# A two-layer mixer/expert kernel on one core: matrices' front with two output buffers, chunk loads in another order, late modulation rows behind the chunks

## What is computed

```python
for i in range(2):                       # layer 0: chunk mixer, layer 1: state-space mixer
    mod_x = silu(c) @ ada_w[i] + ada_b[i]        # six rows of 1024: shift, scale, gate, twice
    mod_c = silu(c_ctx) @ ada_w[i] + ada_b[i]
    xn = rmsnorm(x) * (1 + sc1) + sh1            # cn likewise from the context
    x = x + g1 * mixer(xn)
    x = x + g2 * peer(rmsnorm(x) * (1 + sc2) + sh2)   # 8 heads x 16 experts looked up per token
# state-space mixer: u = xn @ w_in; a diagonal complex scan h_t = a*h_(t-1) + B u_t both ways,
# y = C h + d*u; out = val * sigmoid(gate), [val, gate] = gelu(y) @ w_out
```

## Time and profile before

| | us |
|---|---|
| median of 3 runs (3746.65 to 3755.1) | 3750.82 |
| the profiled execution's own time | 3749.29 |
| its span, first to last instruction | 3747.4 |

### The profile page before, as it was taken

One profiled execution on the slowest core, in us unless ns is written; L12 is line 12 of the kernel. 1 busy time (PEld: TensorE's weight loads), 2 busy tenths in 40 slices (PEclk: granted clock), 3 DMA queues, 4 the chain that ended last, 5 costly groups with the idle time before them and its releaser, 6 DMA issues. The chain is left out here.

```text
span 3747.4 us, 46785 instructions
## 1 busy us (share of the span) xinstructions
PE 3166.1 (84%) x15952; PEld 2087.9 (56%) x15952; DVE 2247.1 (60%) x5038; ACT 1429.8 (38%) x3564; POOL 962.4 (26%) x796
## 2 busy tenths in 40 slices
PE   3886999999988999897766798888877989889897
PEld 2774566554444655442345644444326779777897
DVE  5664766667667666679414466767752259512397
ACT  1222444434334444443224244444432237423275
POOL 0001433434333333344200155444550000000000
PEclk7887999999999999999977899999998989899999
DMA  6746999999999999999967499999992235332353
GB/s 248 277 167 267 418 415 417 421 419 409 421 420 399 409 405 415 415 417 352 369 230 238 163 421 421 421 421 415 415 406 106 90 130 179 135 115 91 129 183 118
DMA packets 177136, 1152.67 MB, mean 308 GB/s; under 512 B 21860, under 2 KB 30264, under 8 KB 43306
## 3 DMA queue, kind: packets, MB, share of 16 engines
q0 software_dynamic: 113936, 827.38, 53.9%
q1 hardware_dynamic: 56058, 304.90, 21.6%
q10 hardware_dynamic: 6944, 17.91, 1.3%
HBM read 1128.86 MB, written 21.25 MB: 307 GB/s over the span
## 5 line engine op out<-in xcount | busy, mean ns | idle before, releaser
L1126 PE MATMUL PS<-AR 128*128 128x512 f32 x3072 | 1511.9, 618 | 249.6 <-ACT AR L1184 241.7
L1311 POOL DMA_INDIRECT AR<-in_peer_uv,AR x768 | 949.2, 1236 | 1514.0 <-PE PS L1126 1109.2
L1287 DVE CUSTOM_DVE_ANT_0 AR<-AR,H 128x1024 f32<-128x1024 f32 x768 | 940.9, 1225 | 655.9 <-DMA AR<-in_peer_uv,AR 636.2
L1126 PEld LDWEIGHTS PS<-AR 128*128 128x128 f32 x3072 | 559.8, 193 | 852.9 <-issue 420.4
L1179 ACT ACTIVATE SM<-SM 128x1 f32<-128x1 f32 x768 | 155.7, 203 | 1130.4 <-DVE SM L1287 1125.3
L1087 PEld LDWEIGHTS PS<-HT,W 128*128 128x128 f32 x1536 | 298.9, 195 | 273.2 <-issue 258.0
L1087 PE MATMUL PS<-HT,W 128*128 128x256 f32 x1536 | 427.6, 387 | 2.7 <-issue 1.3
L1184 ACT ACTIVATE AR<-CON,SM 128x128 f32<-128x128 f32 x768 | 309.1, 402 | 45.6 <-PE PS L1126 21.1
L2578 PE MATMUL PS<-XP,WP 128*128 128x256 f32 x2112 | 264.2, 287 | 22.5 <-DVE WP L2735 15.4
L2578 PEld LDWEIGHTS PS<-XP,WP 128*128 128x128 f32 x2112 | 261.0, 196 | 28.2 <-issue 27.7
L1181 ACT ACTIVATE SM<-SM 128x1 f32<-128x1 f32 x768 | 227.1, 296 | 25.1
(11 more groups left out here) (368 smaller groups left out, 3313.0 us busy)
## 6 DMA issues: line engine op xcount, KB each, us to landing
W<-in_peer_w_q SPq DMA_DIRECT2D x48, 1024.0 KB
W<-in_ada_w SPq DMA_DIRECT2D x32, 1024.0 KB
W<-in_ffn_gate SPq DMA_DIRECT2D x22, 1024.0 KB
W<-in_ffn_val SPq DMA_DIRECT2D x22, 1024.0 KB
W<-in_ffn_out SPq DMA_DIRECT2D x22, 1024.0 KB
W<-in_cm_w_in SPq DMA_DIRECT2D x16, 1024.0 KB
AR<-min_scr SPq DMA_DIRECT2D x16, 1024.0 KB, 9.6
AR<-in_peer_uv,AR POOLq DMA_INDIRECT x768
```

What stands on the lines that cost most here:

```text
L1126: mm = pe.matmul(PS[:, 4 + (u % 2) * 2 + c, :], self.DIAG[:, r % 4, :], self.UV[:, r % RING, D + c * 512:D + (c + 1) * 512], start=(k == 0 ...
L1287: v.tensor_tensor_reduce(rows_, rows_, H[:, self.tb(u), :], 1.0, 0.0, ALU.mult, ALU.add, self.ACTV[:, u % 2, k:k + 1]).then_inc(u_used.sem, 1)
L1311: g.indirect_dma_start(out=self.UV[:, r % RING, :], out_offset=None, in_=t["peer_uv"], in_offset=bass.IndirectOffsetOnAxis(ap=self.IDS[:, ...
```

## The change

Three things in the same program. In the front: MOUT has two buffers, so that DVE waits for the store of chunk c-2; ACT's store waits for the one before; `dve_powers` is cut in two, of which the first goes ahead of `ada0[0].add_bias`; `mixc.act_roots` goes ahead of `mixc.act_in(4)`; the counts of `some` are other; ACT waits for 7 stored MOUTs before `peer0.act`. In the state-space stage, SP issues four chunk loads first and then chunk c+2 behind the matrices of c, and the lag loads of 0 to 2 between. The late rows: pairs 2 and 3 run on PE behind the whole chunk loop, pairs 4 to 7 ahead of `pe_out(4)`; pair 2's load waits for `state_sums` 4; the odd pairs from 3 on lie in W slots 2 and 3, so two of the first four `ssm_w_out` blocks are loaded after the last pair, the others and the `mout_scr` loads no longer wait for it.

```diff
-                self.MOUT = view(0, 2, CG, T8 * GDIM)
+                self.MOUT = [view(18432, 2, CG, T8 * GDIM), view(0, 2, CG, T8 * GDIM)]
...
                 a.wait_ge(self.mout_done, c + 1)
-                a.dma_start(mout_scr[c], self.MOUT.rearrange("p r g x -> p (r g x)")).then_inc(self.mout_out, 16)
+                if c:
+                    a.wait_ge(self.mout_out, c * 16)
+                a.dma_start(mout_scr[c], self.MOUT[c % 2].rearrange("p r g x -> p (r g x)")).then_inc(self.mout_out, 16)
...
                 drain(self.cmul(self.BBR, self.BBI, over_c(self.CO_R), over_c(self.CO_I), self.BR, self.BI, self.T1, self.T2))
+
+            def dve_powers_of(self):
+                L, X1, X2, A_R, A_I, PR, PI = self.link, self.X1, self.X2, self.A_R, self.A_I, self.PR, self.PI
                 L(v.memset(PR[:, 0], 1.0))
...
-                    if c:
-                        v.wait_ge(self.mout_out, c * 16)
+                    if c > 1:
+                        v.wait_ge(self.mout_out, (c - 1) * 16)
...
-        ROW_IN = [XA[:, 2:4, :].rearrange("p t d -> p (t d)"), H[:, 2:4, :].rearrange("p t d -> p (t d)"), view(14464, BLK), view(16512, BLK)]
+        ROW_IN = [XA[:, 2:4, :].rearrange("p t d -> p (t d)"), H[:, 2:4, :].rearrange("p t d -> p (t d)"), view(14464, BLK), view(16512, BLK), W[:, 2, :], W[:, 3, :]]
...
+            @staticmethod
+            def place(j):
+                p = j // 2
+                return ROW_IN[j % 2 + (0 if p % 2 == 0 else 2 if p == 1 else 4)]
+
             def load(self, p):
+                if p == 2:
+                    g.wait_ge(state_sums, 4)
+                    apart(g)
+                if p == 3:
+                    for s in (2, 3):
+                        g.wait_ge(w_used[s], statex.n_in[s] + 2)
+                        apart(g)
+                elif p >= 2:
+                    g.wait_ge(row_used, p - 1)
                 for j in (2 * p, 2 * p + 1):
-                    if j >= 4:
-                        g.wait_ge(row_used, p - 1)
-                    g.dma_start(ROW_IN[j % 4], t["ada_w"][32 + j]).then_inc(row_in[p % 2], 16)
+                    g.dma_start(self.place(j), t["ada_w"][32 + j]).then_inc(row_in[p % 2], 16)
...
-            for c in range(2):
+            for c in range(4):
                 statex.load_chunk(c)
             for c in range(2, NCH):
-                statex.load_chunk(c)
                 statex.load_matrices(c)
-            for c in range(3):
-                outs.load_lags(c)
-            sp.wait_ge(row_used, 8)
+                if c + 2 < NCH:
+                    statex.load_chunk(c + 2)
+                if c > 4:
+                    outs.load_lags(c - 5)
+            sp.wait_ge(row_used, 2)
             for c in range(3):
                 outs.load_out(c)
-            for n in range(4):
+            for n in range(2):
                 outs.load_weight(n)
-            outs.load_gate()
-            for c in range(3, NCH):
+            for c in range(3, NCH // 2):
                 outs.load_out(c)
                 outs.load_lags(c)
+            outs.load_gate()
+            for c in range(NCH // 2, NCH):
+                outs.load_out(c)
+                outs.load_lags(c)
+            sp.wait_ge(row_used, late.PAIRS)
+            for n in range(2, 4):
+                outs.load_weight(n)
...
                 if c + 2 < NCH:
                     statex.pe_turn(c + 2)
-                    late.pe(c + 2)
+            late.pe(2)
+            late.pe(3)
             outs.pe_out(0)
             for c in range(1, NCH):
+                if c == NCH // 2:
+                    for p in range(4, late.PAIRS):
+                        late.pe(p)
                 outs.pe_out(c)
...
             mixc.act_squares()
+            mixc.act_roots()
             drain(mixc.act_in(4))
             matrices(2)
-            mixc.act_roots()
...
+            a.wait_ge(prep.mout_out, 7 * 16)
             peer0.act(fill_act(), rest_of_matrices, first_block_norm())
...
-                if c == 3:
-                    late.store(0)
...
             outs.act_save(0)
-            late.store(1)
+            late.store(0)
...
+                if c == NCH - 2:
+                    late.store(1)
...
+            prep.dve_powers()
             ada0[0].add_bias()
-            prep.dve_powers()
+            prep.dve_powers_of()
...
-            some(40)
+            some(42)
             ada0[1].add_bias()
             mixc.dve_means()
-            some(2)
+            some(1)
             mixc.dve_vars()
-            some(2)
+            some(1)
             drain(mixc.dve_apply(0))
-            some(24)
+            some(30)
             ada0[2].add_bias()
-            some(6)
+            some(4)
...
-                if c == 1:
-                    late.add_bias(0)
...
             outs.dve_scan(0, backward_of)
+            late.add_bias(0)
+            outs.dve_scan(1)
             late.add_bias(1)
-            outs.dve_scan(1)
```

4 lines of the change are left out of this document (2 added, 2 removed).

## The result

The changed kernel takes 3723.86 us (median of 5 runs, 3715.31 to 3729.61), the kernel before 3750.82: a ratio of 0.9927 with an interval of 0.9909 to 0.9945. It is 27 us faster, where 48 were forecast; 3723.86 lies just above the range's end of 3723. The profiled execution has a span of 3721.0 us at a mean clock of 0.936.

What follows compares the result with a forecast made beforehand. It saw the experts' stage as DMA-bound, the front and state stage as chains over engines. Front 25.8 us plus state stage 22.3 us made 48 us off 3749.29, forecast as 3702 us, range 3685 to 3723.

Steps and rivals of the forecast that it cites:

- The frame: Whole kernel: the experts' stage is DMA-bound and moves whole with the front's gain; the state stage's gain adds to it.
- rival E: Experts' stage: its gathers are spaced wider and the kernel gets slower; at 4%, 60 us lost, 3763 us; chance 0.03.
- Front: Start to first gather: 25.8 us saved, from 8.4 for powers, 10.4 for roots and 7 for faster blocks.
- Norm: Front, powers cut in two: DVE's idle time ahead of the first bias is used, the norm starts 8.4 us earlier.
- stall of 10.45: Front, PE ahead of `prep.pe(3)`: with ACT's roots earlier this stall goes whole, 10.4 us.
- the blocks behind it: Front, PE's slow blocks after the stall before `prep.pe(3)` run at fast durations, 7 us saved, bounds 0 and 8.
- Chunks: State stage, ACT's waits for chunk loads: first chunk 5 us sooner, waits under 12 us, scan 0 starts 35 us earlier.
- Scan 0: State stage, DVE: scan 0 with its backwards takes 2 us longer than its 29.9, as loads share the DMA.
- a scan gated by `min_scr`: State stage: a sign that would show the forecast wrong, scan 0 held by the `min_scr` matrices; no size given.
- Late rows: State stage, pairs 4 to 7 ahead of `pe_out(4)`: landings of 6 and 7 put it at 1992, 10.5 us behind DVE's 1981.5.
- Outputs 4 to 7: State stage, end: outputs 4 to 7 and the turns keep their 16.8 us.
- rival B: State stage: late rows slower, `pe_out(4)` at 2004 to 2009, 10 to 15 us less gained, 3712 to 3719; chance 0.15.

Runs made afterwards that it cites:

- e1: The kernel before with only the front's edits (two MOUT buffers, powers cut in two, roots earlier, counts of `some`): 3732.26 us, ratio 0.9941.
- e15: The front's edits alone on the kernel before, but with the powers whole behind the first bias again: 3736.02 us, ratio 0.9957.
- e16: The front's edits alone on the kernel before, but with ACT's roots behind `matrices(2)` again and the old counts of `some`: 3745.03 us, ratio 0.9979.
- e5: The changed kernel with SP issuing the lag blocks of outputs 0 to 2 behind all chunk and input-matrix loads: 3719.17 us, ratio 0.9924.
- e3: The changed kernel without the loads of row pairs 6 and 7 (4 MB), PE computing on old rows: 3714.91 us, ratio 0.9902.
- e11: The changed kernel without the lag-block loads of outputs 3 to 7, computed on old blocks: 3711.36 us, ratio 0.9898.
- e9: The changed kernel with row pair 2 loaded early and used behind pair 1, pairs 5 to 7 ahead of output 4: 3721.34 us, ratio 0.9923.
- e13: As e12, with the first two `ssm_w_out` blocks issued behind the blocks of output 5: 3705.81 us, ratio 0.988.
- e12: The changed kernel with lags 0 to 2 late, pair 2 early, gate load last, pairs 5 and 6 ahead of output 4, 7 behind output 7: 3709.81 us.
- e4: The changed kernel with row pairs 4 and 5 on PE ahead of output 3 instead of output 4: 3722.8 us, ratio 0.9915.
- e6: The changed kernel with row pairs 6 and 7 on PE behind output 7 instead of ahead of output 4: 3722.69 us, ratio 0.9922.
- e8: The changed kernel with lags 0 to 2 late, pairs 6 and 7 behind output 7, pairs 4 and 5 ahead of output 3: 3718.99 us, ratio 0.9915.
- e10: The changed kernel with the load of x's gate issued behind the lag blocks of output 7: 3720.56 us, ratio 0.992.
- e14: As e13, with row pair 5 ahead of output 3 instead of output 4: 3713.06 us, ratio 0.9894.

## Why the prediction was right and wrong

- **The frame held.** The experts' stage moved whole and kept its length (rival E did not occur). What the front gains arrives, as e1 shows by itself.
- **Front: right to 2 us, in part by luck.** 25.8 forecast, 23.4 at the first gather of the changed kernel, 23.5 by the median of the fourteen executions, 21 by e1's median. Norm 8.5 us earlier (8.4), stall of 10.45 gone, the blocks behind it fast. On the way the gain was 16.6 us at the fourth preparation, where powers and roots together were to give 18.8, and 27.0 at the start of the last. Against it stands `matrices(7)`, whose L858 ran 6.87 us at 288.00 where it had run 3.66: 3.2 back, the slow rate turning up elsewhere. Since the same code put the first gather anywhere from 298.7 to 311.6, a hit to 2 us was luck; that the front gains much (16 to 28 us by e1's interval) was not. How it divides into powers and roots is known only to a few us (e15, e16). DVE's waits for MOUT (41.5 us in the earlier trace rows) are gone; what that part is worth by itself was not tried.
- **Chunks: right.** First cut at 1875.36, 4.6 us earlier beyond the shift (5 forecast), all waits for chunks 16.1 us (12 at most forecast; the longest, 7.1, is that of the last chunk and falls behind the start of scan 0), scan 0 36.8 us earlier (35).
- **Scan 0: the first step that failed.** "I add 2 us to scan 0": from its start to that of scan 1 it took 40.9 us, where 31.9 and 0.7 for the bias were forecast. The wait for the matrices behind the chunks, which was to fit into 3 us, was 10.23 for chunk 6 alone. The mechanism was named (a scan gated by `min_scr` as a sign of error) and sized too small. The matrices of chunk 6 were issued 4.1 us late behind 8 lag loads and shared the engines with 4 MB of rows of pairs 2 and 3. e5 takes 6 of the 10.2 us away by the order alone.
- **Late rows: the second, and the larger.** "Pair 6: 1971 + 3 + 10 = 1984 ... Pair 7 ... 1992", 21 us from `late.pe(4)` to output 4. It was 31.5. e3 shows that 20.5 of these are PE's own, so the loads were not alone in deciding. I had counted a pair at 2 x 1.07 to 2 x 1.89 us, 8.6 to 15.1 for four; 7.2 of the 20.5 are stalls without a semaphore in the middle of the blocks. And a block of rows took 10.3 to 17.1 us to land, not the 9.7 of the earlier trace rows, because SP's loads shared the engines: without the lag blocks it was 8.7 to 10.5 (e11). I had named lag blocks and output matrices beside pair 7 and given its load 13 us for them, but pair 6 only 10; pair 6 was used 20.3 us behind `late.pe(4)`, not 13. And pair 7 was issued 7.8 us behind pair 6, not 3, since PE had stalled 4.87 us in pair 5's blocks.
- **Together.** `late.pe(4)` began 1955.55 + 24.2 = 1979.8 on the old clock, 9 us behind my 1971: output 0 came 6.6 us later than forecast, by scan 0, and the pair followed 17.2 us behind it instead of 15; with the 10.5 us of the rows that makes output 4 19.3 us late: 2011.3 instead of 1992. Outputs 4 to 7 kept their length (16.2 us; 16.8 forecast), and the state stage gave 3 us at output 4 instead of 22. That is rival B's mechanism, a little beyond its price (2004 to 2009).
- **How far it is a bound and not two stalls.** From 1872 to 1987 the changed kernel moves 38 x 264 + 28 x 358 + 49 x 280, some 33.8 MB in 115 us; at the 410 GB/s of the gather stage these bytes take 82. By the DMA share the engines were busy for 38 x 0.80 + 28 x 1.02 + 49 x 0.85 = 101 of the 115 us, since with the lag blocks they moved fewer bytes in the same time (the last section). The forecast summed latencies along a chain and never added up the bytes. Taking bytes out of the full stretch shortened the stage (e9 by 7, e11 by 16 us, e13 against e12 by 3.5, the last little more than the scatter); changing only places in PE's queue moved it by less than the scatter (e4, e6, e8). But some 6 us of the wait for chunk 6 do come from SP's order (e5), and e10's shorter waits for rows too, so the bound is not pure.

What stays open: why e14's median is above e13's; the 7 us of stage in e9 that its median does not show; how the 6 to 7 us of e11 divide between the lag blocks and the output matrices that moved with them; what the second MOUT buffer is worth; and how much of PE's stalls in the row blocks is waiting for the DMA engines.

## What to carry to other kernels

When work is moved together so that a chain shortens, add up the bytes of the stretch it is moved into before adding up waits: if the DMA share there is near 1, an instruction's place in PE's queue here moved the wait and hardly the end. Look for loads with a buffer free and nobody waiting soon (here row pair 2 and `ssm_w_out`) and put them into the stretch that is empty. And a gain seen early on a chain is not yet one at its end: in e16's profiled execution 8.5 us at the norm were 1.3 at the third preparation, since the blocks between ran slowly. Before calling a term worth something or nothing, hold the trace of one execution against the median of several.

## What the runs showed of the hardware

**Stalls of PE without a semaphore.** In the row pairs, which are unrolled (128 matmuls of 64 columns a pair, each with its weight load), PE stops in the middle of a block for up to 5.5 us (1.82 and 4.87 in the changed kernel), and often at the same place of the code: after 21 matmuls of pair 3 and 57 of pair 5 in the changed kernel, in e3 and in e11. The DMA view of the changed kernel for 1958.7 to 1963.6, the 4.9 us of one such stall (queue, packets, MB, share of 16 engines), has in it:

```profile
q1 hardware_dynamic: 298, 1.23, 77.7%
q0 software_dynamic: 35, 0.29, 23.8%
q8 instruction: 1, 0.02, 1.4%
```

One packet of the instruction queue passes while PE stands, beside 333 of the two data queues; that it is PE's next code is a reading, not shown. The stall was 4.87 us here and 2.10 at the same place in e11, without the lag blocks. But in e3 one of 3.99 us lies in a stretch with a DMA share of only 0.45, so load alone does not set it. In e3 the four pairs took 20.5 us; counted at 1.07 us per 64 matmuls they would take 8.6, and at 1.89 still only 15.1.

**Loads that cost more than their bytes.** Lag blocks of 64 KB go to 16 partitions each. In the changed kernel the stretch behind output 0 had a DMA share of 0.85 at 280 GB/s. Without them (e11, 1939.9 to 1975) it is:

```profile
1939.90:1975.00 35.10, 21.56 (x728) 19.83 (x729) 21.03 (x117) 17.66 (x28) 2.10 (x4) 0.71 0.78 323
```

More bytes per second at a lower share: 414 GB/s for a full share instead of 329. The DMA view from 1955 to 1970, where the share is 1.03 in the changed kernel and 1.01 in e11, says it directly:

```profile
DMA packets 1022, 4.85 MB, mean 323 GB/s; under 512 B 304, under 2 KB 304, under 8 KB 560
```
```profile
DMA packets 865, 6.33 MB, mean 422 GB/s; under 512 B 94, under 2 KB 94, under 8 KB 94
```

Full engines moved 323 GB/s with the lag blocks (first line) and 422 without. That it is the small packets, and not the 16 partitions or another property of these loads, was not tried.
